# Where the two routing steps of an expert tile stand, and when the first rows of the next product are split

## The reference, cut to what matters

```
e1 = take_along_axis(i1, ci // 16);  e2 = take_along_axis(i2, ci % 16)
eid = e1 * 128 + e2
g = softmax(vs)
a = gelu(einsum('nd,ned->ne', xb, u_tab[eb]))
out = einsum('ne,ned->nd', a * gb, v_tab[eb])
```

## Time and profile before

| | us |
|---|---|
| median of three runs (lowest, highest) | 3994.96 (3989.48, 3998.21) |
| profiled execution, its own time | 3988.7 |
| its span in the trace | 3986.9 |
| routed tiles, from the first matmul of tile 32 to that of the residual | 2678.70 to 2920.56 |

### The profile page before, as it was taken

One profiled execution on the slowest core, in us unless ns is written; L12 is line 12 of the kernel. 1 busy time (PEld: TensorE's weight loads), 2 busy tenths in 40 slices (PEclk: granted clock), 3 DMA queues, 4 the chain that ended last, 5 costly groups with the idle time before them and its releaser, 6 DMA issues.

```text
span 3986.9 us, 82718 instructions
## 1 busy us (share of the span) xinstructions
PE 3939.5 (99%) x33943; PEld 3896.9 (98%) x33943; DVE 2419.8 (61%) x3562; ACT 2005.1 (50%) x3047; POOL 62.6 (2%) x71
## 2 busy tenths in 40 slices
PE   8999999999999999999999999999999999999998
PEld 8999999999999999999999999999999999999998
DVE  7655565575555556555666667987855555555555
ACT  7555554454444444455654544447754444444443
POOL 1000000000000000000000000000000000000000
PEclk9999999999999999999999999999999999999999
DMA  5545555555555555454335544555455556665553
GB/s 212 180 165 175 180 172 196 192 187 193 189 193 196 190 191 184 169 171 147 128 127 197 173 167 151 187 186 184 173 204 194 194 190 216 217 210 190 194 195 126
DMA packets 111190, 726.09 MB, mean 182 GB/s; under 512 B 11297, under 2 KB 11425, under 8 KB 29185
## 3 DMA queue, kind: packets, MB, share of 16 engines
q1 hardware_dynamic: 105904, 701.55, 51.2%
q0 software_dynamic: 5072, 21.50, 1.7%
HBM read 712.52 MB, written 10.49 MB: 181 GB/s over the span
## 4 chain that ended last, share of the span: by engine, by line
PE 90%; DVE 6%; ACT 3%; issue 1%; DMA 0%; DVEq 0%; SPq 0%; ACTq 0%
PE ps L522 18%; PE ps L530 18%; PE ps L523 18%; PE ps L584 9%; PE ps L591 9%; PE ps L586 9%; DVE wl L1811 2%; ACT oh_g L1718 1%; ACT wh L1155 1%; PE ps L551 1%; PE ps L657 1%; PE ps L552 1%; PE ps L556 1%; DVE oh_g L2662 1%; PE ps L676 1%
## 5 line engine op out<-in xcount | busy, mean ns | idle before, releaser
L1811 DVE TENSOR_TENSOR wl<-raw,wh 128x1024 fp32r<-128x1024 f32 x1328 | 1622.9, 1230 | 1363.5 <-ACT wh L1155 1357.8
L1155 ACT ACTIVATE wh<-raw 128x1024 fp32r<-128x1024 f32 x1328 | 1402.0, 1060 | 1775.7 <-PE ps L584 599.3
L522 PE MATMUL ps<-x,wh 128*128 128x256 f32 x6624 | 1570.7, 279 | 6.6 <-DVE x L2272 3.0
L523 PE MATMUL ps<-x,wh 128*128 128x256 f32 x6624 | 1556.2, 277 | 0.0
L522 PEld LDWEIGHTS ps<-x,wh 128*128 128x128 f32 x6624 | 1245.9, 188 | 14.9 <-issue 9.5
L523 PEld LDWEIGHTS ps<-x,wh 128*128 128x128 f32 x6624 | 1245.7, 188 | 0.5
L530 PE MATMUL ps<-x,wl 128*128 128x256 f32 x6624 | 892.7, 277 | 0.3 <-DVE wl L1811 0.3
L530 PEld LDWEIGHTS ps<-x,wl 128*128 128x128 f32 x6624 | 818.8, 188 | 0.5 <-DVE wl L1811 0.5
L584 PE MATMUL ps<-xkh,wh 128*128 128x256 f32 x3328 | 776.3, 276 | 3.1 <-DVE xkl L1822 1.9
L586 PE MATMUL ps<-xkl,wh 128*128 128x256 f32 x3328 | 775.5, 276 | 0.0
L584 PEld LDWEIGHTS ps<-xkh,wh 128*128 128x128 f32 x3328 | 624.6, 188 | 4.7 <-DVE xkl L1822 2.9
(11 more groups left out here) (396 smaller groups left out, 2390.0 us busy)
## 6 DMA issues: line engine op xcount, KB each, us to landing
raw<-in_w_in SPq DMA_DIRECT2D x184, 1024.0 KB, 4.8
raw<-in_expert_u SPq DMA_DIRECT2D x128, 1024.0 KB, 4.8
raw<-in_expert_v SPq DMA_DIRECT2D x128, 1024.0 KB, 4.8
raw<-in_w_ffn_gate SPq DMA_DIRECT2D x44, 1024.0 KB, 4.8
raw<-in_w_ffn_up SPq DMA_DIRECT2D x44, 1024.0 KB, 4.7
raw<-in_w_ffn_down SPq DMA_DIRECT2D x44, 1024.0 KB, 4.7
raw<-in_w_out SPq DMA_DIRECT2D x32, 1024.0 KB, 4.8
raw<-in_w_branch SPq DMA_DIRECT2D x16, 1024.0 KB, 4.9
```

Of the source, the lines that this page charges most:

```text
L522: begin(mm(o, wh[:, j, c], x_h[:, kc, :], start=kc == 0, stop=False), kc % 8 == 0)
L523: mm(o, wh[:, j, c], x_l[:, kc, :], start=False, stop=False)
L1155: f(wh[:, u % 4, 0:width], raw[:, ring, c:c + width], ACT.Copy).then_inc(*k.up("hi"))
L1811: v.tensor_tensor(wl[:, u % 4, 0:width], raw[:, ring, c:c + width], wh[:, u % 4, 0:width].bitcast(F32), ALU.subtract).then_inc(*k.up("lo"))
```

## The change

- TensorE: the two routes of a routed tile are issued between the tile's first and second unit, by the argument `between` that `tile_T` already has. The 24 unread matmuls are gone.
- ScalarE: first unit of tile c+1; for each route `stage_out` and `weigh_hots`; then the wait for the end of tile c, the second unit of tile c+1, the two GELUs and the flag.
- VectorE: first unit of tile c+1; for each route `weigh` and `one_hots`; second unit; the multiplication.
- Tile 63: after the two `weigh`, VectorE raises `early_ready` and both engines split the first two rows of `ag` for the residual, ahead of the second unit and the GELU.
- `gt_row` no longer shares its place with the residual's split rows; it lies in a table of masks that is no longer used.

```diff
             for c in range(HALF):
-                tile_T(c % 2, spare=7 if c == 1 else None)
+                def routes():
+                    for t in range(2):
+                        route(2 * (c - ROUTE_ROW) + t)
+                tile_T(c % 2, spare=7 if c == 1 else None, between=routes if c >= ROUTE_ROW else None)
...
-                if c >= ROUTE_ROW:
-                    for t in range(2):
-                        route(2 * (c - ROUTE_ROW) + t)
-            awake(24, 7)
             residual("v0", HALF)
...
             for c in range(ROUTE_ROW, HALF):
                 i, b = c - ROUTE_ROW, c % 2
                 t = 8 * (i + 1)
-                done(b)
+                half()
+                for n in (2 * i, 2 * i + 1):
+                    stage_out(n)
+                    if n + 2 < 64:
+                        weigh_hots(n + 2)
+                if c == HALF - 1:
+                    early_rows(ag)
+                take(b)
+                half(True)
                 act.wait_ge(*k.next("gate_free"))
                 f(gt_row[:, b, 0:t], ps[:, b, 0:t], ACT.Gelu_apprx_tanh)...
                 if t < T:
                     f(ag[:, c, t:T], ps[:, b, t:T], ACT.Gelu_apprx_tanh)...
                 flag("gate_ready")
-                for n in (2 * i, 2 * i + 1):
-                    stage_out(n)
-                    if n + 2 < 64:
-                        weigh_hots(n + 2)
-            residual(ag, "v0", HALF)
+            residual(ag, "v0", HALF, early=True)
...
             for c in range(ROUTE_ROW, HALF):
                 i = c - ROUTE_ROW
                 t = 8 * (i + 1)
-                split()
+                half()
                 for n in (2 * i, 2 * i + 1):
                     weigh(n, c)
                     if n + 2 < 64:
                         one_hots(n + 2)
+                if c == HALF - 1:
+                    flag("early_ready")
+                    early_rows(ag)
+                half()
                 dve.wait_ge(*k.next("gate_ready"))
                 own()
                 v.tensor_tensor(ag[:, c, 0:t], ag[:, c, 0:t], gt_row[:, c % 2, 0:t], ALU.mult)...
...
-            residual(ag, "v0", HALF)
+            residual(ag, "v0", HALF, early=True)
```

More of the change, by code:

```diff
@@ L255, in build @@
         place("xk", 64, 128)
-        xk0 = nc.sbuf_base
         xkh = sb("xkh", [P, 2, T], F32R)
@@ L352, in build @@
         stage = at("stage", 74, [P, 2, HALF, 16])
-        gt_row = nc.alloc_sbuf_tensor_at("gt_row", [P, 2, T], F32, offset=xk0)
+        gt_row = nd_causal
         gbuf = at("gbuf", 64, [P, 2, 16, P])
```

## The result

The changed kernel takes 4011.23 us (median of 7 runs, 4006.38 to 4012.66) where the kernel before takes 3994.96 (3989.48 to 3998.21): ratio 1.0039, 95% interval 1.0028 to 1.005. Slower was forecast, with 4006.3 us, so 11.3 of slowdown were forecast and 16.3 came. The time lies above the forecast's own range (4003 to 4010) and at the upper edge of the wide one (3995 to 4011).

What follows compares the result with a forecast made beforehand. The prediction took the reordered ScalarE-VectorE loop (7.73 us a tile against TensorE's 7.44) to bound the routed tiles. Residual start 2931.3 + 0.6 - 2920.56 = 11.3 us later, so 3994.96 + 11.3 = 4006.3; own range 4003 to 4010, 8-in-10 range 3995 to 4011.

Steps and rivals of the forecast that it cites:

- The loop: ScalarE and VectorE waiting for each other in routed tiles: 7.36 us before, 3.945 + 1.51 + 1.14 + 1.14 = 7.73 after, against TensorE's 7.44.
- the growth of L2722: VectorE's multiplication in routed tiles grows from 0.17 to 0.43 us, adding up to 0.17 a tile late, 1.4 in all.
- The first routed tile: Tile 32: tables ready no earlier, tile 33 starts 2.87 us later, other engines keep their times, first `weigh` (W) at 2687.65.
- The standstill of 2.94: TensorE in tile 32 wants the routes at about 2681.42 and stands still for 2.94 us.
- The start of the residual: After tile 63: TensorE's first residual matmul comes at W + 2.47 = 2931.3, before any wait for the bank.
- the wait for the bank: Residual's fifth matmul writes the bank tile 63's GELU reads: 0.6 us more waiting, bounds 0 and 1.2.
- The clock: Rival 2: TensorE's clock falls at its two pauses of over 2 us: +14 to +17, 4009 to 4012; chance 0.07.
- The 24 matmuls: Before the residual: removal with early split would give about 3.4 us if TensorE bound, but rows are complete only after the late `weigh`.
- head of the loop: First `weigh` in the routed tiles: VectorE does one unit of 1.14 us instead of two before it, W at 2687.65.
- rival 3: Matmuls in routed tiles get 4 ns closer, 6 us over 31 tiles if rival 1 (loop never closes) holds: 3989; chance 0.05.

Runs made afterwards that it cites:

- run 3: Kernel before with the new order on ScalarE and VectorE and the early row split; TensorE keeps routes at tile end and the 24 unread matmuls: 4007.36 us (1.0025).
- run 5: Changed kernel with two of the four weighting instructions of each route left out, so it computes something else: 3995.17 us (1.0002).
- run 1: Changed kernel with the two routes of tile 32 back at its end; tiles 33 to 63 keep them in the middle: 4006.72 us (1.0027).
- run 2: Changed kernel with 24 unread matmuls ahead of tile 32's routes and the 24 ahead of the residual put back: 4008.54 us (1.0029).
- run 7: Kernel before with one unread matmul of 128 x 384 after each pair of routes: 3995.58 us (1.0001).
- run 6: Kernel before with two of the four weighting instructions of each route left out, as a control: 3989.65 us (0.9994).
- run 4: Kernel before with only TensorE's order changed, the routes in the middle of a tile: 4096.89 us (1.0252).

## Why the prediction was right, and where it was short

- **The loop.** Right, and the main cause (runs 3 and 5). Forecast 7.73 on average with up to 0.17 more in late tiles, measured 7.75 and 7.82. In the changed kernel a second way round is longer by 0.06: ScalarE's unit at 2711.41 starts 0.46 after the second unit on TensorE (2710.95), which follows the last route (2710.07) by 0.88, which follows the weighting (2708.71 + 1.26) by 0.10. With ScalarE to VectorE 1.17, the unit 1.14, and 2.72 or 2.81 to the weighting of 1.28 this gives 7.75 and 7.84. Run 3, without that way, has 7.69 and 7.77. It was not among the links, but hid under an allowance of like size: the growth of L2722 was given up to 0.17 and shows in run 3 as 0.05, in the last nine tiles. The first distance is 0.42 longer, as TensorE comes late from half clock (ScalarE's wait of 0.37 above; 7.74 and 7.75 in runs 1 and 2). Two more take 0.3 longer: VectorE stands still there for 0.39 and 0.46 us and the profile shows nothing on another engine that it waits for. One distance in the kernel before is long too (7.69). The reason was not found. 31 distances: 13.5 more than before, forecast 12.1.
- **The first routed tile.** Here a step failed: "VectorE does one unit instead of two before `weigh`: W is 2686.51 + 1.14 = 2687.65", that is 15.06 from the anchor. It was 17.33. The standstill of 2.94 was right (2.77 of wait), but that ScalarE keeps its times was not. Its unit at 2695.43 overwrites a place that held tile 32's first unit, and this is free only when TensorE has begun tile 32's second unit, which had just been put behind the routes. The description ahead of the prediction hides this: it calls the units that ScalarE and VectorE make beside tile c those of tile c+1, but they are those of tile c+2. Counted in the trace, the one at 2695.43 is ScalarE's 885th, and TensorE's 881st and 882nd are the two of tile 32; with four places, the 885th overwrites the 881st. By the names of the description it would be a unit of tile 33, overwrite one of tile 31, and have nothing to wait for. Runs 1 and 2 share the 2.26 out: 1.56 for that wait, 0.70 for the clock.
- **The start of the residual.** It came 2.35 after the last `weigh` by the trace, forecast 2.47; the wait for the bank was 0.3 (0.51 between two starts, of which 0.21 is a matmul at half clock), forecast 0.6.
- **The clock.** Priced as a rival and given 0.07, it fell at both places in the profiled execution. I put it at "+14 to +17", about 3 to 6 above the forecast. It costs 1.2 up to the last `weigh` (run 2) and 1.25 in the tail (run 1), 2.5 together. That the time came out at +16.3, inside this rival's range, is chance: only half of the 4.7 that were missed is the clock. The ground for the low chance was the idle stretch at the end of the kernel, which was longer than these pauses; that shorter pauses leave the clock alone does not follow from it. It is not certain to fall: with a pause of 2.1 (run 1, at the residual) it stayed.
- **The 24 matmuls.** Their removal wins next to nothing, as forecast, because the rows come later now: by run 2 the start of the residual is 0.6 earlier without them, and the tail 1.7 longer.

By terms against before: head of the loop +1.1 (forecast -1.1), distances +13.5 (+12.1), last `weigh` to residual -0.4 (-0.3), tail +1.8 (bank +0.6): 16.0 against 11.3. The 4.7 that were missed are 2.3 at the head, 1.3 in the distances and 1.2 in the tail, less 0.1; the clock is in all three.

The matmuls did get closer in many tiles of the changed kernel (113 ns, rival 3). As the loop bounds, that only lengthened TensorE's waits. So the direction and most of the size came by the mechanism that was forecast; the head of the loop went the other way than forecast.

## What to carry to other kernels

An engine that is busy for 99% can stand on the edge of a loop between two half-busy ones. Read the distance between the same step in successive tiles and add its links up: if the sum meets the measured distance to the hundredth, the same links in a new order give the least that the new loop takes. It can take more, by a link that was slack before: here the way through TensorE, 0.06 a tile. When a step is moved on one engine, list as well what that engine's later instructions release elsewhere: here not only who waits for the routes, but who waits for the unit that now stands behind them. To find that, count which buffer each instruction overwrites instead of going by its name. A pause of TensorE at the head of such a stage costs what the loop starts later (run 1), not its own length; where TensorE itself is the bound, most of its length is lost (run 5).

## What the runs showed of the hardware

The same fp32 matmuls of 256 columns come 113 ns apart in some stretches and 118 in others at the full clock, with the same busy engines around them. A tile of 48 is then 0.2 us longer. The kernel before was at 113 up to the first routes and at 118 from tile 33 on, through all routed tiles. After one matmul of 384 columns (run 7) it was at 113. In run 6, where TensorE has the same instructions as before, it was at 113 all the way, and in run 3, again with the same instructions, in most tiles. What sets it was not found.

TensorE's clock fell after pauses of 2.8 and 2.2 us, in run 3 after one of 2.0, and in run 5 after the one of 2.2. It did not fall after the pauses of 2.1 at the residual in runs 1 and 5. In run 4 TensorE pauses for some 2 us in each of 31 tiles, and the clock fell four times. The falls near 1553 (three of the ten profiles) and 2416 (eight of ten) also stand right behind places where two matmuls start 1.9 us apart, in the norms ahead of the second block and of the expert layer; the profile of the kernel before has the same gaps and no fall. The fall near 1829 (nine of ten) has no such gap in front. The Trainium skill ("TensorE: Matmul & The Clock Gate", "Why this matters for your kernels") advises against idle gaps between bursts of matmuls, because they bring the clock back down. This trace agrees at both places of the changed kernel, 2.8 and 2.2 us, though these gaps are shorter than those the section warns of; here the measurement decides. What no run settles is why some pauses of 2 us bring a fall and others go by without it.
